# First attention of a two-block transformer in 30 steps of 512 score columns in place of 48 of 128 to 512, with the turn and the values ahead of the scores, and two positions per compression matmul

## The reference

```python
h = rms_norm(x, g_pre_mix) * (1 + sc1) + sh1
proj = h @ w_in                      # queries, keys, indexer, gates
# NSA: 8 heads in 2 groups; DSA: 8 heads on one key head
def compress(kv, pe, w1, w2):        # 31 windows of 32 positions, stride 16
    blocks = kv[:, blk] + pe
    flat = blocks.reshape(B, n_cmp, G, CMP_LEN * dh)
    return gelu(flat @ w1) @ w2      # w1: (32*64) x 128
o_cmp = softmax(q @ k_cmp) @ v_cmp   # masked by window end
o_slc = softmax(q @ ks)    @ vs      # causal, selected blocks (all 8 here)
o_win = softmax(q @ kw)    @ vw      # causal, window of 512
o_nsa = g0 * o_cmp + g1 * o_slc + g2 * o_win
# DSA: the 128 best keys of an index score, then softmax over them
_, sel = top_k(score, 128)
o_dsa = softmax(q_d @ k_d, only sel) @ v_d
o = concat(o_nsa, o_dsa) @ w_out
```

## Time and profile before

| | before |
|---|---|
| median of 3 runs | 1918.88 us (1916.68 to 1921.71) |
| profiled execution, its own time | 1921.35 us |
| its span | 1919.5 us |
| granted TensorE clock, mean | 0.978 |
| TensorE busy | 1828.1 us |
| VectorE busy | 935.1 us |
| ScalarE busy | 697.7 us |
| GpSimd busy | 134.1 us |

### The profile page before, as it was taken

One profiled execution on the slowest core, in us unless ns is written; L12 is line 12 of the kernel. 1 busy time (PEld: TensorE's weight loads), 2 busy tenths in 40 slices (PEclk: granted clock), 3 DMA queues, 4 the chain that ended last, 5 costly groups with the idle time before them and its releaser, 6 DMA issues.

```text
span 1919.5 us, 27690 instructions
## 1 busy us (share of the span) xinstructions
PE 1828.1 (95%) x11652; PEld 1423.4 (74%) x11652; DVE 935.1 (49%) x1482; ACT 697.7 (36%) x1055; POOL 134.1 (7%) x109
## 2 busy tenths in 40 slices
PE   5998989989999998999999999899888899999999
PEld 2666655758888887788888887666688688888887
DVE  4276877364344343544344544545755544433442
ACT  4224557343223233432133334577311433312321
POOL 0013435200000002000000010000000010000000
PEclk8998998989999999999999999999999999999999
DMA  9662101113222223223223322111000122322241
GB/s 380 241 237 105 47 28 34 66 44 99 99 99 96 92 98 99 66 92 129 66 99 107 102 77 77 57 43 44 23 4 4 67 94 93 123 85 88 98 126 40
DMA packets 44475, 176.15 MB, mean 92 GB/s; under 512 B 5568, under 2 KB 5824, under 8 KB 41024
## 3 DMA queue, kind: packets, MB, share of 16 engines
q1 hardware_dynamic: 44352, 174.38, 26.8%
HBM read 168.33 MB, written 2.10 MB: 89 GB/s over the span
## 4 chain that ended last, share of the span: by engine, by line
PE 86%; DVE 7%; ACT 3%; DMA 3%; issue 2%; SPq 0%; DVEq 0%; ACTq 0%
PE bank L365 24%; PE bank L366 23%; PE bank L367 23%; PE bank L509 2%; PE bank L525 1%; PE bank L541 1%; PE bank L716 1%; DMA arena<-ada 1%; PE bank L857 1%; PE bank L874 1%; PE bank L865 1%; DMA arena<-ada_late 1%; PE bank L435 1%; DMA ring<-m_w_v 1%; ACT wsp L1088 1%
## 5 line engine op out<-in xcount | busy, mean ns | idle before, releaser
L1563 DVE TENSOR_TENSOR wsp<-ring,wsp 128x1024 fp32r<-128x1024 f32 (+2 forms) x244 | 313.7, 1287 | 442.6 <-ACT wsp L1088 442.5
L365 PE MATMUL bank<-hs,wsp 128*128 128x512 f32 x1160 | 473.1, 408 | 16.1 <-DVE hs L1830 5.3
L1088 ACT ACTIVATE wsp<-ring 128x1024 fp32r<-128x1024 f32 (+2 forms) x244 | 268.7, 1103 | 579.4 <-PE bank L367 573.7
L367 PE MATMUL bank<-hs,wsp 128*128 128x512 f32 x1160 | 455.5, 393 | 0.0
L366 PE MATMUL bank<-hs,wsp 128*128 128x512 f32 x1160 | 455.3, 393 | 0.0
L365 PEld LDWEIGHTS bank<-hs,wsp 128*128 128x128 f32 x1160 | 220.2, 190 | 87.4 <-issue 31.5
L366 PEld LDWEIGHTS bank<-hs,wsp 128*128 128x128 f32 x1160 | 220.3, 190 | 48.9 <-issue 5.9
L367 PEld LDWEIGHTS bank<-hs,wsp 128*128 128x128 f32 x1160 | 219.7, 189 | 47.2
L365 PE MATMUL bank<-hids,wsp 128*128 128x512 f32 x608 | 236.5, 389 | 0.0
L366 PE MATMUL bank<-hids,wsp 128*128 128x512 f32 x608 | 236.5, 389 | 0.0
L367 PE MATMUL bank<-hids,wsp 128*128 128x512 f32 x608 | 236.5, 389 | 0.0
(11 more groups left out here) (340 smaller groups left out, 2116.0 us busy)
## 6 DMA issues: line engine op xcount, KB each, us to landing
ring<-m_gate SPq DMA_DIRECT2D x44, 512.0 KB, 3.4
ring<-m_up SPq DMA_DIRECT2D x44, 512.0 KB, 3.4
ring<-m_down SPq DMA_DIRECT2D x32, 704.0 KB, 4.1
ring<-m_w_in SPq DMA_DIRECT2D x38, 512.0 KB, 3.5
arena<-ada_late SPq DMA_DIRECT2D x16, 1024.0 KB, 5.8
ring<-m_w_up SPq DMA_DIRECT2D x32, 512.0 KB, 3.4
ring<-m_w_down SPq DMA_DIRECT2D x32, 512.0 KB, 3.4
ring<-m_w_out SPq DMA_DIRECT2D x16, 512.0 KB, 3.6
```

Source lines behind the costliest of these rows:

```text
L365: pe.matmul(out, lhs[0], rhs[0], start=start, stop=False)
L367: return pe.matmul(out, lhs[1], rhs[0], start=False, stop=stop)
L1088: act.activation(wsp[:, s % SPLIT, 0, 0:size], ring[:, i % RING, 0:size], ACT.Copy)\
L1563: dve.tensor_tensor(wsp[:, s % SPLIT, 1, 0:size], ring[:, i % RING, 0:size], wsp[:, s % SPLIT, 0, 0:size].bitcast(F32), ALU.subtract).then ...
```

## The change

1. The pairs are put together in 30 *steps* whose score rows fill a bank of 512 columns: a pair of 512 alone, 384 with 128, 256 with 256. Scores, transposes and values are issued by step. Masks, exp and scaling stay by pair.
2. Beside projection tiles the order is: transposes of step s - 3, values of step s - 4, then scores of s (`CMP_AT` steps: scores between the two). From step `TAIL` = 17 on it is scores, transposes, values. Before the first matmul of a step TensorE waits for both score banks.
3. Steps stand behind two or three k of a tile (`BESIDE`) in place of four. 17 steps (27 pairs) stand beside tiles.
4. ScalarE copies each transposed half bank of 512 alone (60 copies of 512 in place of 72 of 256 to 512).
5. Compression: one matmul takes two positions of 64 rows each, 16 in place of 32, and two weight tiles of 1024 columns in place of three of 1408. For this SP copies the other KV group's half (`swap_halves`), and GpSimd builds the blocks in 16 instructions of 248 columns in place of 8 of 496.
6. `cmp_keys` goes through bank 6 in place of 5. ScalarE's gelu with its two table loads stands in step 1, behind the copy of tile 9 (before: in pair step 2, ahead of it).
7. GpSimd's rotary work for a tile stands in two steps in place of three pairs.

```diff
-        pairs = [(t, br, i) for i in range(4) for br, t in ((0, 3), (0, 0), (0, 2), (0, 1), (1, 3), (1, 0), (1, 2), (1, 1))]
-        pairs += [(t, 2, i) for i in range(4) for t in (3, 0, 2, 1)]
+        for i in range(4):
+            steps += [[(3, 0, i)], [(2, 0, i), (0, 0, i)], [(3, 1, i)], [(2, 1, i), (0, 1, i)], [(1, 0, i), (1, 1, i)]]
+        for i in (0, 2):
+            steps += [[(3, 2, i)], [(2, 2, i), (0, 2, i)], [(1, 2, i), (1, 2, i + 1)],
+                      [(3, 2, i + 1)], [(2, 2, i + 1), (0, 2, i + 1)]]
+        pairs = [pair for step in steps for pair in step]
...
-        CMP_AT = [10, 13, 19, 26]
+        CMP_AT = [4, 7, 13, 17]
+        BESIDE = {9: {3: 0, 7: 1}, 10: {3: 2, 7: 3}, 11: {3: 4, 7: 5}, 12: {2: 6, 5: 7, 7: 8}, 13: {2: 9, 5: 10, 7: 11},
+                  14: {2: 12, 5: 13, 7: 14}, 15: {3: 15, 7: 16}}
+        TAIL = 17
...
-                for l in range(CMP_L):
-                    mm = pe.matmul(bank[:, 6, 2 * CMP_N * m:2 * CMP_N * (m + 1)], ws[l // 11][:, l % 11, :],
+                for l in range(CMP_L // 2):
+                    mm = pe.matmul(bank[:, 6, 2 * CMP_N * m:2 * CMP_N * (m + 1)], ws[l // 8][:, l % 8, :],
...
-                claim(5, "cmp_kv", 1)
+                claim(6, "cmp_kv", 1)
...
+            def qk(s):
+                pe.wait_ge(S("roped"), max((QN + i if br < 2 else KDD) + 1 for t, br, i in steps[s]))
                 for e in range(2):
-                    b = 1 + (2 * p + e) % 3
-                    claim(b, "smin", 2 * p + e + 1)
+                    claim(1 + (2 * s + e) % 3, "smin", 2 * (end_of[s] - 1) + e + 1)
+                for p in range(first_of[s], end_of[s]):
...
+            def attention_step(s):
+                scores_first = s >= TAIL or s in CMP_AT
+                if s < TAIL and 3 <= s:
+                    turn_probs(s - 3)
+                if s == 3:
+                    cmp_keys()
+                if s < NS and scores_first:
+                    qk(s)
+                if TAIL <= s < NS + 3:
+                    turn_probs(s - 3)
+                if s - 4 in CMP_AT:
+                    cmp_out(CMP_AT.index(s - 4))
+                if 4 <= s:
+                    pv(s - 4)
+                if not scores_first:
+                    qk(s)
...
-                if p == 2:
+                if s == 1:
                     act.wait_ge(S("cmp_hid"), 2)
...
-                    for q in range(3):
-                        pair_step(4 * (n - WIDE) + q)
+                    *sooner, after_tile = BESIDE[n].values()
+                    for s in sooner:
+                        attention_step(s)
                 projected(n)
...
+            def swap_halves(m):
+                src = (KC, VC)[m]
+                sy.wait_ge(S("roped"), src + 1)
+                if m:
+                    sy.wait_ge(S("cmp_blocks"), 1)
+                for s in range(2):
+                    sy.dma_start(other_half[DH * s:DH * s + DH, m, :], proj[DH * (1 - s):DH * (1 - s) + DH, src, :])\
+                      .then_inc(S("moved"), 16)
```

More of the change, by code:

```diff
@@ L301, in build, with keys_at, row_of @@
         RW_ORDER = list(range(4, 8)) + [12, 13] + list(range(0, 4)) + list(range(8, 12))
[L303 to L308 removed]
+        steps = []
+        for i in range(4):
[3 more added lines that the diff above has]
+                      [(3, 2, i + 1)], [(2, 2, i + 1), (0, 2, i + 1)]]
+        NS = len(steps)
+        pairs = [pair for step in steps for pair in step]
+        NP = len(pairs)
+        step_of = [s for s, step in enumerate(steps) for pair in step]
+        first_of = [step_of.index(s) for s in range(NS)]
+        end_of = [first_of[s] + len(steps[s]) for s in range(NS)]
+        def keys_at(p):
+            first = first_of[step_of[p]]
+            return sum(t + 1 for t, br, i in pairs[first:p]) * P
+        def row_of(br, i):
+            return i + 4 * (br // 2)
+        LAST_STEP = [max(s for s, step in enumerate(steps) if n in [row_of(br, i) for t, br, i in step]) for n in range(2 * NT)]
+        OPENS = [next(p for p, (t, br, i) in enumerate(pairs) if row_of(br, i) == n) for n in range(2 * NT)]
         def head(br, i, e):
@@ L530, in pv @@
[L530 to L543, removed]
+            def qk(s):
+                pe.wait_ge(S("roped"), max((QN + i if br < 2 else KDD) + 1 for t, br, i in steps[s]))
+                for e in range(2):
+                    claim(1 + (2 * s + e) % 3, "smin", 2 * (end_of[s] - 1) + e + 1)
+                for p in range(first_of[s], end_of[s]):
+                    t, br, i = pairs[p]
+                    at, kv = keys_at(p), (t + 1) * P
+                    for e in range(2):
+                        mm = pe.matmul(bank[:, 1 + (2 * s + e) % 3, at:at + kv],
+                                       proj[DH * e:DH * e + DH, (QN, QN, QD)[br] + i, t * P:(t + 1) * P],
+                                       proj[DH * e:DH * e + DH, (KSL, KW, KDD)[br], 0:kv], start=True, stop=True)
+                        if p + 1 == end_of[s]:
+                            mm.then_inc(S("scores"), 1)
@@ L1189, in outputs, with probs_turned @@
[L1189 to L1204, removed]
+            def probs_turned(s):
+                if s >= 2:
+                    act.wait_ge(S("pv"), s - 1)
+                for e in range(2):
+                    act.wait_ge(S("probs_turned"), 2 * s + e + 1)
+                    act.activation(probT[s % 2][:, e, :], bank[:, 4 + e, :], ACT.Copy).then_inc(S("probT"), 1)
@@ L1786, in cmp_probs @@
                 own("cmp_probs")
+            begins = {next(iter(at.values())): n for n, at in BESIDE.items()}
             for p in range(NP + 1):
+                s = step_of[p] if p < NP else NS
+                closes = p < NP and p + 1 == end_of[s]
                 if p < NP:
@@ L1811, in _ @@
                     rounds += 1
+            outputs(2 * NT - 2)
             outputs(2 * NT - 1)
```

222 lines of the change are left out of this document (108 added, 114 removed).

## The result

The changed kernel takes 1932.23 us, median of five runs (1928.32 to 1937.39), against 1918.69 us (1913.96 to 1921.71) for the kernel before, run beside it: ratio 1.0073, 95% interval 1.0049 to 1.0098. The forecast was 1901 us, range 1889 to 1914. The profiled execution took 1928.32 us.

A forecast was written before the change was run, and what follows sets the result against it. The prediction took TensorE, busy 95% of the span, as the bound wherever no other engine holds it up, with VectorE close behind from 190 to 281. Terms -3.7 - 9.3 - 2 - 3 = -18 us gave 1901 us, range 1889 to 1914.

The forecast's parts named there:

- term 2: Opening, 149 to 190 us: -9.3 us, the idle time of VectorE, taken as smaller than TensorE's 13.6.
- Keys' compression: Compression of the keys, where TensorE is the limit: 16 matmuls in place of 32 save 3.7 us.
- rival B: The opening's holes come back elsewhere and only the two compressions count, 7.4 us: 1911.5 us, chance 0.19.
- 190 to 281: Stretch from 190 to 281 us: double steps save fixed parts of blocks, half counted, -2 us (bounds -4.2 and +4.2).
- The hole at 284.62: TensorE's 3.81 us wait for ScalarE's copy of turned compressed probabilities stays, at step 20: 0 us.
- DSA: DSA part, 294 to 342.5 us: fewer fixed parts and bank waits, half of 5.6 us taken, -3 us.
- A: TensorE is the limit throughout, so all its savings count, 27 us: 1892 us, chance 0.20.
- D: VectorE's chain alone sets the stage, begins 3.7 us earlier and finds its waits again: 1915 us, chance 0.10.
- Rival C: VectorE starves because scores come after transposes and values in 14 steps, losing 28.6 us: 1929.5 us, chance 0.06.

The follow-up runs named there:

- e1: The changed kernel with 128 unused bytes behind the column table, so later tiles start where they did in the kernel before: 1913.27 us, ratio 0.9969.
- e2: The kernel before with 128 unused bytes behind the column table, moving its later tiles off multiples of 256: 1939.82 us, ratio 1.0108.
- e4: The changed kernel with the tile arena alone aligned to 256 bytes, ext and tmp left where the change put them: 1915.01 us, ratio 0.9980.
- e5: The kernel before with the tile hs alone moved 128 bytes off a multiple of 256, arena still on one: 1937.87 us, ratio 1.0095.
- e6: The kernel before with only the new compression, cmp_keys left in bank 5, later tiles kept at their places: 1914.89 us, ratio 0.9980.
- e7: e1 without the 32 search rounds inside the attention stage, so the DSA selection is not computed: 1892.52 us, ratio 0.9852.
- e8: The kernel before without the 32 search rounds inside the attention stage, so the DSA selection is not computed: 1904.12 us, ratio 0.9924.
- e10: e1 with scores, then transposes, then values in every step, as in the kernel before: 1907.24 us, ratio 0.9933.

## Why the prediction was wrong

**The step that failed** is the last sentence of the prediction: "or if the parts after it changed: they have the same lists". The lists are the same and the parts changed, by 15.5 us in the trace, because a place in memory is no part of a list. e1, e2, e4 and e5 show it from both sides. The diff held what was needed; I priced instructions only. With that put right the change gives 0.9969, 6 us, where 18 were forecast, so a second step failed too: term 2, which took VectorE's idle time for time that can be had. The terms:

1. *Keys' compression, -3.7: right.* 3.6 us in the trace, -3.8 for the whole compression in e6.
2. *Opening, -9.3: mis-sized, -1.0.* The first mask of the second head pair stood at 193.88 and stands at 187.73: 6.15 us earlier, of which tile 8 brought 5.15. The named holes did go. But the list that I took for the limit, VectorE's, was not free to use what it had idled: in step 4 TensorE waited 4.92 us for a mask behind the copies of the keys and two search rounds, then ran at half clock, and VectorE waited 1.76 and 3.16 us for what came late by that and by the new order. That is what rival B named, and its 1911.5 us lies by e1's 1913.27; the closeness is in part luck, for B counts 7.4 us for the compression, of which e6 shows 3.8. The granted clock from 172 to 190 is 0.81, as before, where near 1.00 was expected.
3. *190 to 281, -2: the size about right.* The first DSA mask came 9.14 us earlier (296.67, 287.53), 3.0 more than at the start of the stretch. But TensorE waits for masks there, up to 3.7 us at once, which I had not listed: I looked at VectorE's waits for TensorE and not at TensorE's for VectorE.
4. *The hole at 284.62, 0: right,* 3.90 us at step 20 (284.53), and half clock behind it.
5. *DSA, -3: mis-sized, about +1.* The fixed part is saved: a free step takes 3.17 us, five of them 15.9 in place of 18.7 for two head pairs; 1.6 of these 2.8 us are the two waits of 0.82 between heads, which are gone too. In the second two (303.38 on) the 3.77 us for a mask, with VectorE at the split of a weight tile, and half clock took it back; the whole stage ended 8.4 us earlier, having been 9.1 ahead.

The Trainium skill (TensorEngine Tiling (Array Packing), Key Properties) says that a change of tiling mode drains TensorE, and by that each block saved is time. The trace agrees that a block has a fixed part: scores of 384 and 128 in one block take 1.07 us (300.21 to 301.28), where two blocks took 0.85 and 0.43 by the prediction's count. That a drain is what costs it, no run shows. And e7 against e8 shows the time come out, 14 us, once VectorE has room. With the search rounds in place less than half of it does. So of the rivals A fell for this kernel; D's 1915 lies close too, but D has VectorE find its waits again, and these are 15.3 us ahead of its masks in e1 where they were 23.6.

**Rival C** gave 1929.5 us, near the 1932.23 measured by accident: VectorE's waits ahead of its masks shrank from 23.6 to 13.2 us, and the loss came from an address. Its mechanism was there in a small size: scores last cost 7 us (e10 against e1), not 28.6.

So the parts, in us of the median: compression -3.8; steps of 512 with scores first, with all other parts of the change, about -9 (e10's -12.9 less that); scores last +7; place of `arena` +19. They are differences along one chain of runs (before, e6, e10, e1, changed), so that they sum to the measured 13.5 (1932.23 - 1918.69) is no proof of them.

## What to carry to other kernels

Whenever an edit changes the size of any table, compare the start addresses of every tile behind it, and fix those that matmuls stream from to a multiple of 256 bytes (64 and 128 bytes off were tried here, and both cost); a row such as 395 ns for 389 of the same form, in a part nobody touched, is the sign. TensorE, busy 95%, still gained only what VectorE beside it let through: read the waits in both directions, and price a shorter list in a stage by the other one's list. Where another engine lives on one kind of result, issue that kind first.

## What the runs showed of the hardware

- A float32r matmul of 128x512 took 389 ns in the records with its moving operand at a multiple of 256 bytes and 395 at 128 off, 6.7 ns apart by the rate of 24. All three products paid at 128 off. At 64 off the three took 395, 392 and 389. At 128 off it cost this kernel 1.0 to 1.1%, at 64 off 0.65%.
- The same for `hs`: 391 and 397 ns, 0.95% of this kernel.
- A hole of 4.9 us on TensorE was followed by half clock (0.63 us for 0.39 a matmul, 0.81 granted from 172 to 190), so it cost more than its length.
